# Modulation of the last gate moved from the prompt attention into the output projection of a decoder layer, and squares of two norms added up on VectorE

## The reference, cut to what matters

```
mod = silu(c) @ w_ada + b_ada                       # w_ada is 2048 x 12288, c has 9 rows
shift1, scale1, gate1, shift2, scale2, gate2 = split(mod, 6)
h = rmsnorm(x) * (1 + scale1) + shift1
p = h @ w_in                                        # projections for two attentions and merge gates
m = sigmoid(gA) * (nsa_attention @ w_a) + sigmoid(gB) * (dilated_attention @ w_b)
x = x + gate1 * (m @ w_out)                         # output projection
h = rmsnorm(x) * (1 + scale2) + shift2
x = x + gate2 * ((silu(h @ w_gate) * (h @ w_up)) @ w_down)
y = rmsnorm(x)
```

## Time and profile before

| | |
|---|---|
| Median of 3 runs | 2208.37 us (2204.28 to 2209.1) |
| Profiled execution | 2213.8 us, span 2212.0 us |
| Granted TensorE clock, mean | 0.958 |
| Busy: PE / PEld / DVE / ACT | 91% / 83% / 44% / 35% |
| Prompt attention, modulation steps | about 550 to 714 us |
| Output projection | about 1263 to 1364 us |
| Down projection | about 1902 to 2190 us |

### The profile page before, as it was taken

How to read it: one execution, slowest core, us unless ns; L and a number is a source line. 1 busy time by engine, 2 the same in 40 slices (tenths; PEclk the granted TensorE clock), 3 DMA queues, 4 the chain that set the end, 5 groups by cost and what they waited for, 6 DMA issues and landing times.

```text
span 2212.0 us, 36599 instructions
## 1 busy us (share of the span) xinstructions
PE 2017.2 (91%) x15699; PEld 1841.2 (83%) x15699; DVE 971.0 (44%) x1697; ACT 766.5 (35%) x1214; POOL 66.0 (3%) x116
## 2 busy tenths in 40 slices
PE   6988999999899596878999997999999999999968
PEld 4567999999454464668999996999999999999967
DVE  3354455543544421116444565444434444644425
ACT  2354333334343220105333433433333333533312
POOL 0000000000000010000000000000000000000010
PEclk9998999999999897889999998999999999999989
DMA  9962769898999284555655654577677766577782
GB/s 374 422 241 72 252 219 286 279 287 282 421 420 403 83 304 175 183 162 184 197 171 183 206 165 152 190 248 246 244 256 239 265 234 232 174 251 259 251 285 81
DMA packets 344728, 529.77 MB, mean 239 GB/s; under 512 B 9025, under 2 KB 318569, under 8 KB 327065
## 3 DMA queue, kind: packets, MB, share of 16 engines
q1 hardware_dynamic: 323586, 369.01, 50.0%
q0 software_dynamic: 6400, 142.51, 16.6%
q10 hardware_dynamic: 14640, 16.80, 2.3%
HBM read 521.54 MB, written 98.91 MB: 280 GB/s over the span
## 4 chain that ended last, share of the span: by engine, by line
PE 80%; DMA 13%; DVE 5%; ACT 2%; issue 1%; SPq 0%; DVEq 0%; ACTq 0%
PE bank L1033 17%; PE bank L1034 17%; PE bank L1035 17%; DMA piece<-in_w_ada 8%; PE bank L809 5%; PE bank L810 5%; PE bank L811 5%; PE bank L699 2%; PE bank L736 2%; DMA piece<-in_w_down 2%; PE bank L958 1%; PE bank L928 1%; DMA mem<-in_cache_win_kv 1%; PE bank L990 1%; PE bank L918 1%
## 5 line engine op out<-in xcount | busy, mean ns | idle before, releaser
L1033 PE MATMUL bank<-piece,piece 128*128 128x264 f32 x3072 | 880.6, 287 | 54.9 <-DVE piece L1895 26.3
L1034 PE MATMUL bank<-piece,piece 128*128 128x264 f32 x3072 | 876.7, 285 | 0.0
L1035 PE MATMUL bank<-piece,piece 128*128 128x264 f32 x3072 | 876.2, 285 | 0.0
L1900 DVE TENSOR_TENSOR piece<-piece,piece 128x2048 fp32r<-128x2048 f32 (+2 forms) x216 | 440.7, 2053 | 543.3 <-ACT piece L1419 543.3
L1033 PEld LDWEIGHTS bank<-piece,piece 128*128 128x128 f32 x3072 | 581.9, 189 | 56.9 <-DVE piece L1900 24.2
L1035 PEld LDWEIGHTS bank<-piece,piece 128*128 128x128 f32 x3072 | 582.0, 189 | 0.0
L1034 PEld LDWEIGHTS bank<-piece,piece 128*128 128x128 f32 x3072 | 581.5, 189 | 0.5
L1419 ACT CAST piece<-piece 128x2048 fp32r<-128x2048 f32 (+2 forms) x216 | 368.6, 1715 | 602.6 <-PE bank L1035 520.5
L809 PE MATMUL bank<-piece,piece 128*128 128x264 f32 (+1 forms) x816 | 240.5, 295 | 0.0
L810 PE MATMUL bank<-piece,piece 128*128 128x264 f32 (+1 forms) x816 | 234.7, 288 | 0.0
L811 PE MATMUL bank<-piece,piece 128*128 128x264 f32 (+1 forms) x816 | 234.5, 287 | 0.0
(11 more groups left out here) (300 smaller groups left out, 1560.3 us busy)
## 6 DMA issues: line engine op xcount, KB each, us to landing
piece<-in_w_ada SPq DMA_DIRECT2D x48, 2048.0 KB, 12.9
out_s_dil<-in_cache_dil_kv POOLq DMA_DIRECT2D x64, 1023.5 KB, 6.2
piece<-in_w_in SPq DMA_DIRECT2D x50, 1024.0 KB, 8.1
piece<-in_w_gate SPq DMA_DIRECT2D x22, 2048.0 KB, 8.1
piece<-in_w_up SPq DMA_DIRECT2D x22, 2048.0 KB, 8.1
piece<-in_w_down SPq DMA_DIRECT2D x32, 1408.0 KB, 7.1
piece<-in_w_in SPq DMA_DIRECT2D x16, 2048.0 KB, 8.0
piece<-in_w_out SPq DMA_DIRECT2D x8, 2048.0 KB, 8.3
```

What stands on the lines that cost most here:

```text
L1033: mm(out, w_high[:, k, :], half_tile(x_high[k]), start=(start and k == first_tile), stop=False)
L1034: mm(out, w_high[:, k, :], half_tile(x_low[k]), start=False, stop=False)
L1035: last = mm(out, w_low[:, k, :], half_tile(x_high[k]), start=False, stop=(stop and k == len(x_high) - 1))
L1900: v.tensor_tensor(half_chunk(a, k_tiles, f, CW), raw, half_chunk(buffer, k_tiles).bitcast(F32), ALU.subtract)\
```

## The change

The sixth block of the modulation is no longer made in the prompt attention: 24 of the 40 units have a step, not 32. It is made in the output projection instead, in 16 steps of one K tile (1 MB of w_ada, two buffers, 4 matmuls), one behind each of the 16 products. The loads for it stand in SP's program behind the four loads of each round. ScalarE copies the result behind the last step, before `ffn_first`; PE turns it before the FFN; VectorE adds the bias in `norm("n2")`. The products of the output projection rotate over 6 banks, not 7. The three page loads of GpSimd wait for the last three of the 40 steps.

In both later norms VectorE adds the squares of the 16 tiles into one (`rstd`), and PE multiplies the sum by the matrix of ones once.

```diff
-    NA = ADA_PARTS * ADA_STEPS
+    LATE = ADA_PARTS - 1
+    NA = LATE * ADA_STEPS
+    gate2_at = [oN0, region + (KT + 4) * T + 16 * T]
...
                 sp.dma_start(slot(s), rows(w_out, slice((4 * i + s) * CW, (4 * i + s + 1) * CW))).then_inc(w_ld["wout"][s], 16)
+            for k in range(8 * i, 8 * i + 8):
+                if k == 0:
+                    sp.wait_ge(mg_half, 48)
+                if k >= 2:
+                    sp.wait_ge(*pe_.at("gate2", k - 2))
+                sp.dma_start(at_words(gate2_at[k % 2], D), w_ada[k * P:(k + 1) * P, LATE * D:(LATE + 1) * D])\
+                    .then_inc(*gate2_in[k % 2].mark("w", k, by=16))
...
-                    split_products(bank[n % 7][:, 0:T], slot_at(s), wout_high[n % 4], f, KT, x_high[0:KT], m_low,
+                    split_products(bank[n % 6][:, 0:T], slot_at(s), wout_high[n % 4], f, KT, x_high[0:KT], m_low,
                                    True, True, "m_low" if n == 0 else None).then_inc(wo_half, 1)
-                    if n >= 4:
-                        stat("n2", n - 4)
-        for k in range(12, KT):
-            stat("n2", k)
+                    pe.wait_ge(*gate2_in[n % 2].at("w", n))
+                    for j in range(4):
+                        last = mm(bank[6][32 * j:32 * j + 32, :], siluP[:, n, :], at_words(gate2_at[n % 2] + j * 512, 512),
+                                  start=(n == 0), stop=(n == KT - 1))
+                    last.then_inc(*pe_.mark("gate2", n))
+        pe.wait_ge(*dve_.at("sum", "n2"))
+        mm(bank[7][:, 0:T], ones, rstd, start=True, stop=True).then_inc(*pe_.mark("sum", "n2"))
+        pe.wait_ge(*act_.at("ada_row", LATE))
+        pe.wait_ge(*dve_.at("residual", KT - 1))
+        for f in range(4):
+            last = turn(bank[5][:, f * P:(f + 1) * P], ada_row[:, LATE % 2, f * P:(f + 1) * P], ident)
+        last.then_inc(*pe_.mark("ada_turn", LATE))
...
+        act.wait_ge(*pe_.at("gate2", KT - 1))
+        cp(ada_row[:, LATE % 2, :], bank[6][:, :]).then_inc(*act_.mark("ada_row", LATE))
+
         def ffn_first():
...
-                square("n2", j)
+                if j == 0:
+                    v.tensor_tensor(rstd, xT[:, j, :], xT[:, j, :], ALU.mult).then_inc(*dve_.mark())
+                else:
+                    link(v.tensor_tensor(tmp[:, 0, :], xT[:, j, :], xT[:, j, :], ALU.mult))
+                    v.tensor_tensor(rstd, rstd, tmp[:, 0, :], ALU.add).then_inc(*dve_.mark(*(("sum", "n2") if j == KT - 1 else ())))
...
-            last_stat(i + (-1), 1)
             down(i, 1, False)
-            last_stat(i, 0)
-        last_stat(3, 1, stop=True)
+        pe.wait_ge(nf_sum, 16)
+        mm(bank[7][:, 0:T], ones, rstd, start=True, stop=True).then_inc(nf_total, 1)
...
+                v.tensor_tensor(tmp[:, 0:1, :], xT[:, one, :], xT[:, one, :], ALU.mult).then_inc(nf_sq, 1)
+                dve.wait_ge(nf_sq, i * 4 + (2 * u + f + 1))
+                dve.wait_ge(nf_sum, i * 4 + (2 * u + f))
+                v.tensor_tensor(total, total, tmp[:, 0:1, :], ALU.add).then_inc(nf_sum, 1)
```

More of the change, by code:

```diff
@@ L206, in piece, with at_words @@
         return pieces[a, words, dtype]
+    def at_words(a, words):
+        return mem[:, a:a + words]
     top = [0]
@@ L323, in program @@
     prod = mem[:, region + KT * T:region + (KT + 4) * T].rearrange("p (j t) -> p j t", t=T)
-    xs8 = rstd[:, 0:B].unsqueeze(1)
+    xs8 = facA[:, 0:1, 0:B]
     mT = mem[:, region:region + KT * T].rearrange("p (j t) -> p j t", t=T)
@@ L338, in program @@
     h_high = tiles_at((oN0, 12), (spare + 4096, 4))
-    siluP = part(KT * 32).rearrange("p (k c) -> p k c", c=32)
+    siluP = part(KT * 32, WORDS - KT * 32).rearrange("p (k c) -> p k c", c=32)
+    assert top[0] <= WORDS - KT * 32 and ffn_high[2] + 2048 <= WORDS - KT * 32
     ADA_PARTS, ADA_K = 6, 2
     ADA_STEPS = KT // ADA_K
-    NA = ADA_PARTS * ADA_STEPS
+    LATE = ADA_PARTS - 1
+    NA = LATE * ADA_STEPS
+    gate2_at = [oN0, region + (KT + 4) * T + 16 * T]
     ADA_FIRST = 2
@@ L414, in program @@
     caches_copied = signal("caches_copied")
+    gate2_in = [signal(f"second_gate_weights{s}_in") for s in range(2)]
     ada_in = [signal(f"ada_weights{s}_in") for s in range(4)]
@@ L422, in program @@
     ff_high, ff_low, ff_half = sem("ffn_high_parts"), sem("ffn_low_parts"), sem("ffn_halves_used")
-    nf_sq, nf_used = sem("last_norm_squares"), sem("last_norm_squares_used")
+    nf_sq, nf_sum, nf_total = sem("last_norm_squares"), sem("last_norm_summed"), sem("last_norm_total")
     dn_high, dn_low, dn_half = sem("down_high_parts"), sem("down_low_parts"), sem("down_halves_used")
@@ L611, in gathers @@
                 elif u < B + 3:
-                    pool.wait_ge(*pe_.at("ada", {2: NA - 3, 0: NA - 2, 1: NA - 1}[s]))
+                    pool.wait_ge(*pe_.at("ada", {ada_slot(a): a for a in range(NA - 3, NA)}[s]))
                 else:
@@ L665, in _ @@
             turn(z[:, TP:T], x_ts[0:B, k * P:(k + 1) * P], ident[0:B, 0:B]).then_inc(*pe_.mark("xT", k))
-        def stat(tag, k):
-            pe.wait_ge(*dve_.at("sq", tag, k))
-            mm(bank[7][:, 0:T], ones, tmp[:, k % 4, :], start=(k == 0), stop=(k == KT - 1)).then_inc(*pe_.mark("sq", tag, k))
         pe.wait_ge(vec_loaded, 4 * 16)
@@ L1068, in _ @@
                     pe.wait_ge(wo_low, n + 1)
-                    if n >= 7:
-                        pe.wait_ge(wo_kept, n - 6)
+                    if n >= 6:
+                        pe.wait_ge(wo_kept, n - 5)
                     elif n == 2:
                         pe.wait_ge(mg_t, 32)
-                    split_products(bank[n % 7][:, 0:T], slot_at(s), wout_high[n % 4], f, KT, x_high[0:KT], m_low,
+                    split_products(bank[n % 6][:, 0:T], slot_at(s), wout_high[n % 4], f, KT, x_high[0:KT], m_low,
                                    True, True, "m_low" if n == 0 else None).then_inc(wo_half, 1)
-                    if n >= 4:
-                        stat("n2", n - 4)
-        for k in range(12, KT):
-            stat("n2", k)
+                    pe.wait_ge(*gate2_in[n % 2].at("w", n))
[10 more added lines that the diff above has]
+        last.then_inc(*pe_.mark("ada_turn", LATE))
         h_low = tiles_at((hT0, KT))
@@ L1093, in ffn @@
                                    True, True, "h_low" if first and s == f == 0 else None).then_inc(ff_half, 1)
+        pe.wait_ge(*dve_.at("mod", LATE))
         ffn(0, True)
@@ L1107, in down @@
                                    f"f_low{s}" if very_first and f == 0 else None).then_inc(dn_half, 1)
[L1109 to L1113, removed]
         down(0, 0, True, True)
         down(0, 1, True)
-        last_stat(0, 0, start=True)
         with pe.Fori(1, 4) as i:
             down(i, 0, False)
-            last_stat(i + (-1), 1)
             down(i, 1, False)
-            last_stat(i, 0)
-        last_stat(3, 1, stop=True)
+        pe.wait_ge(nf_sum, 16)
+        mm(bank[7][:, 0:T], ones, rstd, start=True, stop=True).then_inc(nf_total, 1)
         for k in range(KT):
@@ L1574, in ada_mod @@
                 .then_inc(*dve_.mark("mod", part_))
[L1575 to L1578, removed]
         def mean_square(tag):
@@ L1638, in norm @@
             if tag == "nf":
-                dve.wait_ge(nf_used, 16)
+                dve.wait_ge(nf_total, 1)
                 mean_square(tag)
             elif tag == "n2":
-                dve.wait_ge(*pe_.at("sq", tag, KT - 1))
+                dve.wait_ge(*pe_.at("sum", tag))
                 mean_square(tag)
+                j16 = slice(LATE * KT, (LATE + 1) * KT)
+                dve.wait_ge(*pe_.at("ada_turn", LATE))
+                v.tensor_tensor(modT[:, j16, :].rearrange("p (j f) c -> p j f c", f=4),
+                                bank[5][:, :].rearrange("p (f j c) -> p j f c", f=4, j=4)[:, :, :, 0:9],
+                                biasT[:, j16].rearrange("p (j f) -> p j f", f=4).unsqueeze(3).broadcast_to([P, 4, 4, 9]), ALU.add)\
+                    .then_inc(*dve_.mark("mod", LATE))
             if shift is not None:
@@ L1958, in _ @@
                     dve.wait_ge(wo_kept, j)
-                residual(j, bank[j % 7], 2, wo_t, 2 * (j + 1), wo_kept)
+                residual(j, bank[j % 6], 2, wo_t, 2 * (j + 1), wo_kept)
+                dve_.marks["residual", j] = dve_.n + 1
                 dve.wait_ge(wo_kept, j + 1)
-                square("n2", j)
+                if j == 0:
[3 more added lines that the diff above has]
+                    v.tensor_tensor(rstd, rstd, tmp[:, 0, :], ALU.add).then_inc(*dve_.mark(*(("sum", "n2") if j == KT - 1 else ())))
         for n in range(4):
@@ L2007, in down_low, with down_residual @@
                             .then_inc(*dve_.mark(f"f_low{s}", k))
-        def down_residual(c, kept_before, squares_before=True):
+        def down_residual(c, kept_before):
             i, u = c
@@ L2017, in down_residual, with down @@
                 dve.wait_ge(dn_kept, i * 4 + (2 * u + f + 1))
-                if squares_before:
```

(20 more changed lines are left out.)

## The result

The changed kernel takes 2236.03 us, the kernel before 2208.02 (medians of 4 runs each). The ratio is 1.0114, 95% interval 1.0088 to 1.014: 25 us slower by the ratio, 28 by the medians, where 13 were forecast and the range ended at 2232. The direction was right, the size was not. The profiled execution has a span of 2234.6 us, 22.6 more than that of before.

The account below looks back on a forecast made before the run. The prediction took TensorE as the bound (80% of the chain, transfers 13%), with VectorE and ScalarE pacing attention units without steps. It summed -13.5 + 27.4 + 2.5 - 3.4 = +13.0 onto 2208.4, giving 2221.4 us, range 2205 to 2232.

Parts of the forecast that it names:

- Part 1: Prompt attention: units 24 to 31 without steps take 32 us instead of 45.45, a gain of 13.5 us.
- rival C: Attention: less busy TensorE loses clock, its 2.7 us double, gain only 2 us; +24.5, 2232.9 us in all; chance 0.08.
- Part 2: Output projection: sixteen steps enter and the `stat` matmuls leave; the end of product 15 moves 27.4 us later.
- The first wait: Output projection, behind product 0: TensorE waits 7.0 us for the first K tile, queued behind w_out slots 2 and 3.
- the second: Output projection, behind product 8: TensorE waits 8.3 us for K tile 8, queued behind the second round of w_out loads.
- the upper bound that I had named: Output projection: if a 2 MB load takes 6 us of the queue, the stage's delay is 30 us.
- The wait ahead of product 8: Output projection, second round: TensorE waits 1.4 us until product 8 can start on its w_out weights.
- A step: Output projection: each K tile costs TensorE 0.9 us with its start; steps 1 to 14 add 12.6 us.
- The clock behind the waits: Output projection: lower TensorE clock after each of the two long waits costs 1.7 us each, 3.4 in all.
- Part 3: Between the last product and the FFN: the last step and ScalarE's copy make this stretch 2.5 us later.
- part 4: Down projection: fewer `stat` matmuls save 4.45 us, VectorE's last additions cost 1.0; net gain 3.4 us.
- Rival A: Output projection: the loads are not late, TensorE pays only its own work; -5.9, 2202.5 us in all; chance 0.13.

Follow-up runs that it names:

- fill_one: The changed kernel plus four 128x512 float32 matmuls on constants, products unused, in each of attention units 24 to 31; ratio 1.0104 to the kernel before.
- queue_order: The changed kernel with SP's loads of w_ada, w_out and first FFN weights issued in the order they come due; ratio 1.0005 to the kernel before.
- no_steps: The changed kernel without the 16 w_ada loads and without modulation steps 0 to 14 in the output projection; ratio 0.9942 to the kernel before.
- sums_only: The kernel before with only the squares added on VectorE and one matmul of ones per norm, modulation unmoved; ratio 0.9973 to the kernel before.
- sums_again: The same code as sums_only, run once more; ratio 0.9964 to the kernel before.

## Why the prediction was wrong

**Part 1, the attention: the step that failed.** I let the loop over VectorE and ScalarE set the pace because "TensorE's own part between two units ... is 2.7 us, so it fits under the loop". That price held at a granted clock of 1.00, and it was the removed steps that held the clock there. At 0.50 it is 4.8 us and over the loop (3.56 and 4.18 us). Of 13.5 us the profile shows 3.3: eight units in 38.2 instead of 45.45, less 2.5 in the dilated units, which start cold (36.2 us to the kept keys instead of 33.7), and 1.5 by which the first 24 were longer. The other kernels with this attention gain 7.0 to 7.5. This was my rival C, to which I gave 0.08. I had set the dilated units against it, which were busy 24.9 of 30 us at full clock. That was one stretch that was already warm, and it did not tell for NSA units: in the changed kernel the same dilated units, again without steps, start at 0.50 and have 1.00 from 722 us on, where the NSA units ahead of them stay low. fill_one shows the cause, since adding work takes the loss away, and the two halves of queue_order's units show the price of the clock alone.

The Trainium skill ("TensorE: Matmul & The Clock Gate", HAM oscillation — how this bites in real kernels) describes loops in which waits bring the clock down again and again. The traces here agree in that the clock falls in a loop with waits, to 0.50 to 0.62 in the windows above. They differ in the waits: in queue_order those of TensorE ahead of the fall are 0.58 to 1.61 us, for VectorE and not for transfers.

**Part 2, the output projection: right mechanism, three terms too small.** It moved by 34.7 us, not 27.4.

- The first wait was worked out as 7.0 and measured as 7.2; the second as 8.3 and measured as 10.3. In the second round the four loads of w_out landed 6.1, 6.9 and 5.2 us apart, 6.1 in the mean and not 5.3: about the upper bound that I had named. K tile 8 landed 2.5 us behind them, as worked out.
- The wait ahead of product 8 was worked out as 1.4 and measured as 1.2.
- A step costs 1.18 us in line (no_steps: 1.19), not 0.9. I had read the length of a step, and not what the change of matmul form costs the product behind it. The length was read too short as well: I took 0.2 us off the 1.92 as run-out, but in the earlier trace rows the next instruction starts 1.86 us behind the step's start, 0.93 for a tile. For steps 0 to 14 this makes 4.2 us more.
- The clock behind the waits: step 0 took 0.95 us more and product 1, up to step 1 at 1275.1, took 7.8 instead of about 6.0; behind the second wait it was 0.95 and 0.8. That is 4.5, not 3.4.

These differences, 0.2 + 2.0 - 0.2 + 4.2 + 1.1, are the 7.3 us.

**Part 3** was 2.2 us (2.5 forecast), **part 4** 2.9 in the profile (3.4 forecast), where sums_only and sums_again have 2.2 and 3.0. sums_only confirms the 5.0 us of the `stat` matmuls. Rival A, loads that are not late, is what queue_order made true by hand; then part 1 and the price of the steps leave no gain either, where I had counted one of 5.9.

The measured change is 12 us above the forecast by the ratio and 15 by the medians. Part 1 holds 6 to 10 us of it and part 2 seven, which together is 13 to 17; what is over or missing lies within the noise of the profiles. Left open is what exactly decides between the warm and the cold state of a unit without filling: in queue_order the first of them ran warm, in the changed kernel the clock was down from 677 us on, about one unit after the steps ended.

## What to carry to other kernels

Before work is taken from an engine whose clock depends on how busy it is, price what remains at both clock levels, and test with useless work in its place. In the output projection the large loads of one queue landed in the order of issue: write that order by the time at which each is wanted, and put a load that waits for a late step behind those that do not. When transfers bound some units and not their neighbours, spreading the same bytes over more units can give the gain of moving them elsewhere, without its price.

## What the runs showed of the hardware

Useless matmuls made a stage shorter: 188.7 us with eight groups of four 128x512 float32 matmuls, 194.5 to 198.7 without. Going from such matmuls, in four groups of 32 columns, back to full float32r matmuls costs the chain 0.2 us each time. SP's own issue of a load took 0.4 us into a queue with little ahead and 3.9 us for slot 3 of the second round, with several megabytes ahead. It did not delay the load behind it here: K tile 8 was issued 3.9 us later and still landed only 2.5 us behind slot 3, the time of its own 1 MB.
